# Attention stage of a two-block transformer kernel: the last weight splits cut into quarters, a later turn of the probabilities, and the first half of the output added in two places

## The reference, cut to what matters

```python
for l in range(DEPTH):                                   # DEPTH = 2
    x = x + 0.5 * swiglu(rms_norm(x, norm_ffn1[l]), ...)
    x = x + hybrid_mixer(rms_norm(x, norm_mix[l]), w_in[l], ..., w_out[l], cos, sin)
    x = x + 0.5 * swiglu(rms_norm(x, norm_ffn2[l]), ...)

def hybrid_mixer(h, w_in, ..., w_out, cos, sin):
    proj = h @ w_in
    # 8 "NSA" heads: compressed, selected and windowed attention, three outputs per head
    o_nsa = g0 * o_cmp + g1 * o_slc + g2 * o_win         # g = sigmoid(gates)
    # 8 "MoBA" heads; with 256 positions and blocks of 256 it is plain causal attention
    return concatenate([o_nsa, o_moba]) @ w_out
```

## Time and profile before

| | before |
|---|---|
| median of 3 runs (range) | 2482.06 us (2478.13 to 2487.17) |
| the profiled execution's own time | 2482.52 us |
| its span in the trace | 2480.7 us |
| TensorE busy | 91% of the span |
| VectorE, ScalarE busy | 57%, 40% |
| mean share of the DMA engines used by loads | 38.6% |
| granted TensorE clock, mean | 0.94 of full speed |
| loop of 48 units, first layer | about 286.9 to 421 us |
| the same loop, second layer | about 631.1 to 631.2 us later |

### The profile page before, as it was taken

How to read it: one execution, slowest core, us unless ns; L and a number is a source line. 1 busy time by engine, 2 the same in 40 slices (tenths; PEclk the granted TensorE clock), 3 DMA queues, 4 the chain that set the end, 5 groups by cost and what they waited for, 6 DMA issues and landing times. The chain is left out here.

```text
span 2480.7 us, 39201 instructions
## 1 busy us (share of the span) xinstructions
PE 2264.3 (91%) x15940; PEld 2101.9 (85%) x15940; DVE 1411.5 (57%) x2036; ACT 989.5 (40%) x1308; POOL 18.8 (1%) x18
## 2 busy tenths in 40 slices
PE   6997999899799899989959989988997989988997
PEld 6997976799799798679949979978996979987997
DVE  5544452654555345365537566567765856656765
ACT  4333342533433234343335423335444533334552
POOL 0000000000000000000000000000000010000000
PEclk9998996899899899689979989998998999998999
DMA  7435310742544342055334322237434322235551
GB/s 272 186 135 180 124 52 1 280 180 108 199 194 159 127 176 69 1 229 203 135 118 157 109 72 94 94 102 278 173 119 168 137 75 77 94 103 205 198 190 53
DMA packets 79564, 349.01 MB, mean 141 GB/s; under 512 B 21184, under 2 KB 30528, under 8 KB 45504
## 3 DMA queue, kind: packets, MB, share of 16 engines
q1 hardware_dynamic: 79424, 347.07, 38.6%
HBM read 345.99 MB, written 1.05 MB: 140 GB/s over the span
## 5 line engine op out<-in xcount | busy, mean ns | idle before, releaser
L88 PE MATMUL bank<-ffn_hT_split,ffn_split_weights 128*128 128x256 f32 x1408 | 402.5, 286 | 11.0 <-DVE ffn_hT_split L174 11.0
L89 PE MATMUL bank<-ffn_hT_split,ffn_split_weights 128*128 128x256 f32 x1408 | 402.2, 286 | 0.0
L90 PE MATMUL bank<-ffn_hT_split,ffn_split_weights 128*128 128x256 f32 x1408 | 402.0, 285 | 0.0
L88 PEld LDWEIGHTS bank<-ffn_hT_split,ffn_split_weights 128*128 128x128 f32 x1408 | 274.0, 195 | 14.1 <-DVE ffn_hT_split L174 12.7
L89 PEld LDWEIGHTS bank<-ffn_hT_split,ffn_split_weights 128*128 128x128 f32 x1408 | 274.0, 195 | 1.4
L90 PEld LDWEIGHTS bank<-ffn_hT_split,ffn_split_weights 128*128 128x128 f32 x1408 | 274.1, 195 | 0.0
L88 PE MATMUL bank<-conv_ffn_hT_split,conv_ffn_split_weights 128*128 128x256 f32 x704 | 201.8, 287 | 5.5 <-DVE conv_ffn_hT_split L174 5.5
L89 PE MATMUL bank<-conv_ffn_hT_split,conv_ffn_split_weights 128*128 128x256 f32 x704 | 201.5, 286 | 0.0
L90 PE MATMUL bank<-conv_ffn_hT_split,conv_ffn_split_weights 128*128 128x256 f32 x704 | 201.3, 286 | 0.0
L339 DVE TENSOR_TENSOR ffn_split_weights<-ffn_arrived_gate_up,ffn_split_weights 128x2048 fp32r<-128x2048 f32 x84 | 188.8, 2288 | 21.4 <-ACT ffn_split_weights L269 21.4
L1441 DVE TENSOR_TENSOR mix_parts<-mix_arrived,mix_parts 128x1024 fp32r<-128x1024 f32 x88 | 107.3, 1224 | 137.5 <-ACT mix_parts L1436 137.3
(11 more groups left out here) (354 smaller groups left out, 5741.6 us busy)
## 6 DMA issues: line engine op xcount, KB each, us to landing
ffn_arrived_gate_up<-in_ffn SPq DMA_DIRECT2D x88, 1024.0 KB, 8.2
ffn_arrived_down<-in_ffn SPq DMA_DIRECT2D x44, 1024.0 KB, 4.9
mix_arrived<-in_mix_w SPq DMA_DIRECT2D x88, 512.0 KB, 3.5
conv_ffn_arrived_gate_up<-in_conv_ffn SPq DMA_DIRECT2D x44, 1024.0 KB, 6.7
rw_project_arrived<-in_w_in SPq DMA_DIRECT2D x34, 1024.0 KB, 4.9
mixer_arrived<-in_w_in SPq DMA_DIRECT2D x22, 1024.0 KB, 6.6
conv_ffn_arrived_down<-in_conv_ffn SPq DMA_DIRECT2D x22, 1024.0 KB, 4.9
mixer_arrived<-in_w_out SPq DMA_DIRECT2D x8, 1024.0 KB, 4.9
```

Source lines behind the costliest of these rows:

```text
L88: pe.matmul(out, lhs[0], rhs[0], start=start, stop=False)
L89: pe.matmul(out, lhs[0], rhs[1], start=False, stop=False)
L90: return pe.matmul(out, lhs[1], rhs[0], start=False, stop=stop)
```

## The change

It does five things in the loop. (1) Each of the seven 128 x 2048 splits of the loop is cut into four quarters of 512 columns. ScalarE does one quarter per step in four steps in a row, VectorE its quarter one step later each time; unit 15 begins at step 47 in place of 48. (2) `turn`, `copy_probs` and `add` run one step later: `turn(u-3)`, `add(u-4)`, with a fourth buffer for the exponents; the loop has one more step. (3) The steps of `READ_AT`, `SUM_AT`, of the second and third entry of `O_TURN` and of `moba(0)` are moved by one or two steps to follow. (4) The output rows of tile 0 are done half by half (`k` 0 to 3 of half 0, then of half 1), and each half is added to the residual on its own, at steps 39 and 43, where both were added at step 43. (5) The last output row of tile 1 that stood behind the loop moves into step 51.

```diff
     def high(self, eng, n, width=UNIT, part=None):
...
+        cols = slice(0, width) if part is None else slice(part * width // 4, (part + 1) * width // 4)
+        eng.activation(self.parts[:, 0, n % RING, cols], self.arrived[:, n % RING, cols], ACT.Copy
+                       ).then_inc(self.s["unit_high"], 4 if part is None else 1)
...
+        eng.wait_ge(self.s["unit_high"], 4 * n + (4 if part is None else part + 1))
...
+        if part in (None, 3):
+            last.then_inc(self.s["unit_split"], 1)
...
+    LAG = 3
...
-    probs = [scratch(S) for _ in range(3)]
+    probs = [scratch(S) for _ in range(LAG + 1)]
...
-    O_TURN = {31: 0, 39: 1, 46: 2}
-    READ_AT = {11: (0, 1), 16: (0, 0), 19: (0, 2), 27: (1, 1), 29: (1, 0), 35: (1, 2)}
+    O_TURN = {31: 0, 40: 1, 47: 2}
+    READ_AT = {12: (0, 1), 17: (0, 0), 20: (0, 2), 28: (1, 1), 30: (1, 0), 36: (1, 2)}
...
-    SUM_AT = {21: 0, 37: 1}
-    OUT_STEPS = {34 + n: (0, n // 2, n % 2) for n in range(8)} | {44 + n: (1, n // 2, n % 2) for n in range(7)}
+    SUM_AT = {22: 0, 38: 1}
+    OUT_STEPS = {34 + n: (0, n % 4, n // 4) for n in range(8)} | {44 + n: (1, n // 2, n % 2) for n in range(8)}
+    SPLIT_AT = {u + q: (jobs[job][0] + RING, q) for u, job in ENDS_AT.items() if job == last_job[jobs[job][0]] for q in range(4)}
+    SPLIT_AT |= {47 + q: (N_UNITS - 1, q) for q in range(4)}
+    N_STEPS = N_ATT + LAG + 1
...
-                if u >= 3:
-                    act.wait_ge(s["p_turned"], u - 2)
+                if u > LAG:
+                    act.wait_ge(s["p_turned"], u - LAG)
...
-                if 2 <= u < N_ATT + 2:
-                    copy_probs(u - 2)
-                if u in ENDS_AT:
-                    high_after(ENDS_AT[u])
+                if LAG <= u < N_ATT + LAG:
+                    copy_probs(u - LAG)
+                if u in SPLIT_AT:
+                    unit, part = SPLIT_AT[u]
+                    ring.high(act, unit, width(unit), part)
...
-                if u - 1 in ENDS_AT:
-                    low_after(ENDS_AT[u - 1])
+                if u - 1 in SPLIT_AT:
+                    unit, part = SPLIT_AT[u - 1]
+                    ring.low(dve, unit, width(unit), part)
...
-                if u == MOBA + NH + 3:
+                if u == MOBA + NH + LAG + 2:
                     moba(0)
...
-                if u == 43:
-                    for half in range(2):
-                        cols = slice(half * 512, half * 512 + 512)
-                        dve.wait_ge(s["nsa_out"], half + 1)
-                        dve.tensor_tensor(c.x[:, 0, cols], out_bank(0, 0, half)[:], c.x[:, 0, cols], ALU.add
-                                          ).then_inc(s["nsa_added"], 1)
...
+                if u in (39, 43):
+                    half = (u - 39) // 4
...
-                if 2 <= u < N_ATT + 2:
-                    turn(u - 2)
-                if u >= 3:
-                    add(u - 3)
+                if LAG <= u < N_ATT + LAG:
+                    turn(u - LAG)
+                if u > LAG:
+                    add(u - LAG - 1)
...
-            out_rows(1, 3, 1)
```

More of the change, by code:

```diff
@@ L500, in load, with high @@
         sp.dma_start(self.arrived[:, n % RING, 0:width], src).then_inc(self.s[f"unit{n % RING}"], 16)
-    def high(self, eng, n, width=UNIT, on_pool=False):
+    def high(self, eng, n, width=UNIT, part=None):
         eng.wait_ge(self.s[f"unit{n % RING}"], 16 * (n // RING + 1))
@@ L543, in first_map @@
     c.wc1 = at("w_cmp1", 4096, [P, 2, CJ, CMP_HID])
[L544 to L545 removed]
+    c.attention = at("attention", 4096, [P, 10 * S + N_WORK])
+    c.branch_rows = at("branch_rows", 4096 + 10 * S + N_WORK, [P, 3, Q_COLS])
     c.wc2 = at("w_cmp2", 12288, [P, 2, 2, 2, DH])
@@ L636, in scratch @@
         return c.attention[:, at - n:at]
+    units = attention_units()
+    N_ATT = len(units)
+    LAG = 3
     scores = [scratch(S) for _ in range(3)]
-    probs = [scratch(S) for _ in range(3)]
+    probs = [scratch(S) for _ in range(LAG + 1)]
     probsT = [scratch(S) for _ in range(3)]
@@ L650, in nsa_phase @@
     KV_K, KV_V, CMP_S = 128, 192, 256
-    units = attention_units()
-    N_ATT = len(units)
     NSA_T = 2 * NH
@@ L796, in _ @@
                            ACT.Gelu_apprx_tanh).then_inc(s["gelu_ready"], 1)
-            for u in range(N_ATT + 3):
+            for u in range(N_STEPS):
                 if u in ENDS_AT:
@@ L810, in _ @@
                     o_high(O_TURN[u - 1])
-                if u == 48:
-                    ring.high(act, N_UNITS - 1, width(N_UNITS - 1))
             o_high(3)
@@ L1002, in _ @@
                     o_low(O_TURN[u - 2])
-                if u == 43:
-                    for half in range(2):
-                        cols = slice(half * 512, half * 512 + 512)
-                        dve.wait_ge(s["nsa_out"], half + 1)
-                        dve.tensor_tensor(c.x[:, 0, cols], out_bank(0, 0, half)[:], c.x[:, 0, cols], ALU.add
-                                          ).then_inc(s["nsa_added"], 1)
-                if u == 49:
-                    ring.low(dve, N_UNITS - 1, width(N_UNITS - 1))
+                if u in (39, 43):
+                    half = (u - 39) // 4
+                    cols = slice(half * 512, half * 512 + 512)
+                    dve.wait_ge(s["nsa_out"], half + 1)
+                    dve.tensor_tensor(c.x[:, 0, cols], out_bank(0, 0, half)[:], c.x[:, 0, cols], ALU.add
+                                      ).then_inc(s["nsa_added"], 1)
             moba(1)
```

19 lines of the change are left out of this document (6 added, 13 removed).

## The result

The changed kernel takes 2453.15 us in the median of 4 runs (2433.3 to 2466.07), the kernel before beside it 2482.34 (4 runs): ratio 0.9864, interval 0.9834 to 0.9894. That is 29 us less by the two medians and 34 by the ratio. The forecast was 14 less. The sign and the places were right, the size was not. The four times, 2433.3, 2449.97, 2456.34 and 2466.07, go with the mean granted clock of each run, 0.955, 0.950, 0.947 and 0.944. The profiled execution is the fastest, 2433.30 us; where its stretches of clock are read, the spread of the other runs has to be kept in mind.

The account below looks back on a forecast made before the run. The loop was held to be bound by TensorE's half-clock stretches and its waits. From 2482.5 us, -4.9 for waits and small terms and -8.6 for one long stretch make -13.5, so 2469, stated as 2468; range 2450 to 2479.

Parts of the forecast that it names:

- Removes no wait: Turn one step later: the turn still waits for ScalarE's copy, so cost and gain 0.
- 8.6 us for a stretch of 20.5: Price of each long slow-clock stretch in the loop, taking 42% of slow time as lost.
- I give each first stretch one chance in five to vanish: Long slow stretch beginning after the waits of steps 32 and 33, one per layer; 8.6 us each.
- 1.3 of the four in the mean: Long slow stretches expected to vanish over both layers, at 8.6 us each; one the likeliest number.
- the 0.82: TensorE's wait in us ahead of the turn of step 23, taken to show such a wait can be enough.
- it is only avoided if the clock is already back: Second long stretch, at step 44: vanishes only if full clock has returned by steps 42 and 43; chance 0.45.
- -4.9 in all: Waits and small terms of both layers, -2.45 us each; bounds -9 to 0.
- -1.1 for the waits: Steps 41 to 44, per layer: the 1.50 us wait at step 44 goes, some 0.4 is given back.
- +1.1: Second turn of `o` one step later (40): one more slow step per layer, in us.
- rival 3: Three or four long slow stretches vanish: -30.7 to -39.3 us, so 2443 to 2452; chance 0.13.
- Rival 4: Slower: 28 quarter steps each delay mask and TensorE by 0.3 us, 2494 us in all; chance 0.10.
- The rule of small waits: Number of small TensorE waits counts, not only the longest; slow stretches would stay, leaving the sum at -4.9 us.

Follow-up runs that it names:

- Filling the second place alone: Kernel before with 7 identity matmuls ahead of the output row of step 44 alone; 2463.36 us, ratio 0.9912.
- the repeated kernel: The changed kernel measured once more with no edit; 2444.98 us, ratio 0.9858.
- the first place of the kernel before filled: Kernel before with identity matmuls in its waits of steps 23, 32, 33 and 34 alone; 2462.73 us, ratio 0.9910.
- with its waits filled: Kernel before with identity matmuls in its five waits (steps 23, 32, 33, 34, 44), nothing else changed; 2445.29 us, ratio 0.9848.

## Why the prediction was right and wrong

**Right: the bound and the mechanism.** The loop was held by waits and by slow clock, and the large term is the clock. The changed kernel has, as the forecast said, no wait at the turns of steps 31 to 33, one at the turn of step 24 (0.54 for about 0.9), VectorE's sum behind the rotation (343.55), one ahead of the first output row (1.00 for 1.2 to 1.3), one at step 42 (0.36 for 0.4), and none ahead of the output row of step 44. "Removes no wait" for the later turn is shown by the kernel with the turn two behind.

**Right, a size: "8.6 us for a stretch of 20.5".** Filling the second place alone takes 8.36 and 8.68 us out of the two loops, with no wait shortened, and all the slow clock of a loop is worth 18.66 where the forecast's terms make 2 x 8.6 + 1.4 = 18.6. The share of 42% came from one kind of step, with a row's cost at full clock from another place (at full clock that step now takes 2.15 and not 2.26); that it holds so closely for the mixture of steps is in part luck. The Trainium skill, page "TensorE: Matmul & The Clock Gate", section "HAM oscillation — how this bites in real kernels", reckons the loss of throttled time as that time by one minus the ratio of the clocks, which is 10.25 for 20.5. The traces here show less, 8.4 to 8.7 for 20.5 and 20.85 for 47.8, though TensorE was busy for nearly all of each stretch.

**Wrong, the step that decides: "I give each first stretch one chance in five to vanish", and "1.3 of the four in the mean".** In the profiled run all four went; in the profile of the repeated kernel both of the second layer did, and in the first layer one stretch of 47.8 us covered the two places. From the times, as an estimate: ten runs of the changed kernel have a mean of 2449.6 us. That is 16.3 above the profiled run with no stretch, or 1.9 stretches left at 8.6; and it is 32.7 below the kernel before, of which 8.1 are the new order and 2.8 the two short stretches, so that 21.8 or 2.5 stretches are gone. So 2.1 to 2.5 of the four went where the forecast had 1.3; the two estimates differ since time outside the loops scatters too. I took the length of the waits for what counts, and held the 0.82 that came ahead of a short fall as proof that 1.2 would do. A wait of 1.0 us stands there now, and in six of eight loops no stretch begins at it. I also let the second stretch hang on the first ("it is only avoided if the clock is already back"). That happens: the stretches of 47.8 and 51.2 us ran over the second place. But with a first stretch of 20.5 and the second place filled there was no second one, so this is no rule.

**Wrong, a second size: the waits and small terms, "-4.9 in all".** Of this, -2.8 are the two short stretches, and -2.1 the new order, 1.05 per layer; measured, the new order is worth up to 4.04 per layer. Up to the first output row the forecast had 1.05: the way there from the first score takes 85.59 us with the first place of the kernel before filled (286.59 to 372.18) and 82.93 in the changed kernel. Of these 2.66, 0.70 are no gain, since with the turn two behind the way is 83.63 and the loop as long; 1.96 are left. Behind the row the forecast had nothing net: -1.1 for the waits and "+1.1" for the late turn of `o`. Measured it is 4.04 less 1.96, or 2.1. There was no slow stretch for the late turn to lengthen, and the 0.4 that step 42 was to give back stood there before (397.42). With -10.9 the term lies outside its bounds of 0 to -9.

Together: 8.1 of the order, 2.8 of the short stretches and 2.1 to 2.5 long ones at 8.6 make 29 to 32 us, against the measured 29 to 34. With all four gone the forecast's terms give 39.3 (rival 3); the profiled run is 49.2 below, and of the 9.9 between them 4.2 are time outside the loops and the rest, near enough, the order.

**Rival 4** (masks held up by the cost of small operations) did not come: 28 quarters cost 0.46 us more per split on VectorE and, where the forecast took 0.45, 0.58 on ScalarE, and of the 28 steps TensorE waits over 0.3 us in two alone, 24 and 34; the one that a late mask makes, step 24, is the one I named. The dearer small pieces are there; they did not reach the path.

**The rule of small waits.** The reading I gave of the Trainium skill ("TensorE: Matmul & The Clock Gate", section "A second HAM failure mode: psum-queue depth-cycling"), that the stretches stay as long as small waits are left, does not hold as such: three waits were left and most stretches went. But the kernel with the tile turned at step 30 speaks for its core where I weighed only the longest wait: no wait over 0.51, and slow stretches of 51.2 us in both layers. No run separates the number of the waits from their place.

## What to carry to other kernels

A wait of TensorE that costs a microsecond can cost eight or nine more, and over twenty where the stretch is long: look at the granted clock behind each wait, and price a slow stretch from the same rows at either clock (here a little over four tenths of its length, not half). Measure a loop from its own first row, since slow clock ahead of it moves all absolute times. Before rearranging work to remove such a wait, fill it with idle matmuls: it costs a line, shows what the clock is worth there, and may be the better fix; what the waits themselves cost is still there to be won by a better order (up to 4 us per loop here). Where runs of one kernel scatter by more than 1%, compare each time with its mean granted clock first, and judge by medians of several runs; a single profile shows one outcome of several.

## What the runs showed of the hardware

The same program at the same waits takes 2433.3 or 2469.8 us, and the longer time goes with the lower mean granted clock (0.955 and 0.942). The kernel before lay between 2477.01 and 2484.4 in the 17 runs of one comparison and between 2473.81 and 2501.39 in those of another; with its waits filled it stayed within 7 us. In the loops of these profiles a slow stretch, once begun, ended after 3.4, 10.2, 17.1, 20.5, 23.9, 27.3, 47.8 or 51.2 us; in the two of 51.2 at the tile turned at step 30, TensorE was busy for 50.9 of 51.2 us and was not given the full clock back, while in the kernel before it was after 20.5. The fall came within the wait (399.9, ahead of the row at 400.89) or up to 1.9 us after its end (1020.3, behind the row at 1018.39 in the second layer of the kernel before filled to 34). What decides this was not found. Nor is the length of a wait the measure of its danger: one of 1.0 us ahead of full rows (369.25) was harmless in six of eight loops, one of 0.35 was the only one near a fall (387.3, the turn two behind), and two of 0.43 and 0.44 us, 1.2 us of work apart, were followed by a fall in both layers, and with them the 12 runs had a median of 2472.85.
